# Query and forget tiles of a recurrent layer: the activations' high part and remainder as one wide operand, the two sums added by VectorE

## What is computed

```python
def hgrn2_mixer(h, w_in, lb, norm_g, w_out):
    u = h @ w_in
    q, fz, i, gate = jnp.split(u, 4, axis=-1)          # 256 x 2048 each
    log_f = jnp.logaddexp(jnp.log(lbf), jnp.log1p(-lbf) + jax.nn.log_sigmoid(fz))
    k = (1.0 - lbf) * jax.nn.sigmoid(-fz)
    ...
    # o_t = S_t^T q_t  with  S_t = diag(f_t) S_{t-1} + k_t v_t^T, in chunks
    o = hgrn2_chunk_scan(qc, kc, vc, bc)
    o = o * lax.rsqrt(jnp.mean(o * o, axis=-1, keepdims=True) + EPS)
    return (o * norm_g * jax.nn.silu(gate)) @ w_out
```

## Time and profile before

| | |
|---|---|
| median of 3 runs | 821.23 us (820.32 to 822.46) |
| the profiled execution | 821.18 us |
| its span | 819.9 us |
| TensorE busy | 801.5 us, 98% |
| VectorE busy | 627.7 us, 77% |
| ScalarE busy | 474.4 us, 58% |
| granted TensorE clock, mean | 0.997 |

### The profile page before, as it was taken

The page is one execution under the profiler, slowest core; times in us unless marked ns, Lnnn a source line. Parts: engine busy times, 40 slices in busy tenths (PEclk is TensorE's granted clock), DMA queues, the critical chain, the costliest instruction groups (busy, mean ns, idle before and its releaser), DMA issues.

```text
span 819.9 us, 12702 instructions
## 1 busy us (share of the span) xinstructions
PE 801.5 (98%) x5059; PEld 687.6 (84%) x5059; DVE 627.7 (77%) x939; ACT 474.4 (58%) x811; POOL 40.6 (5%) x52
## 2 busy tenths in 40 slices
PE   8999989999999999999999999999999999999996
PEld 5999978888998999999987789886476888888885
DVE  6786667747689889899795885898759877767775
ACT  6564444355667877868856551547636654455443
POOL 6010001700000000000000000000000000000000
PEclk9999999999999999999999999999999999999999
DMA  8989966594543444545346772936647655655631
GB/s 276 324 263 252 265 201 239 221 307 141 173 150 118 142 152 154 155 155 181 130 156 240 273 260 77 378 113 232 202 156 234 203 183 177 204 184 179 204 103 51
DMA packets 105701, 160.05 MB, mean 195 GB/s; under 512 B 11317, under 2 KB 74137, under 8 KB 103338
## 3 DMA queue, kind: packets, MB, share of 16 engines
q1 hardware_dynamic: 105642, 159.24, 59.1%
HBM read 156.02 MB, written 3.21 MB: 194 GB/s over the span
## 4 chain that ended last, share of the span: by engine, by line
PE 88%; DVE 6%; DMA 3%; ACT 2%; issue 1%; SPq 0%; DVEq 0%; ACTq 0%
PE acc L472 9%; PE acc L473 9%; PE acc L474 9%; PE acc L493 9%; PE acc L524 8%; PE acc L526 8%; PE acc L525 8%; PE acc L494 4%; PE misc L1322 3%; PE misc L2331 3%; PE misc L2333 2%; PE misc L2332 2%; PE misc L923 2%; DMA raw<-in_pool_w_in_dram 1%; PE acc L497 1%; PE misc L650 1%
## 5 line engine op out<-in xcount | busy, mean ns | idle before, releaser
L445 DVE TENSOR_TENSOR w_lo<-raw,w_hi 128x2048 fp32r<-128x2048 f32 x113 | 260.9, 2320 | 62.0 <-ACT w_hi L438 61.9
L438 ACT ACTIVATE w_hi<-raw 128x2048 fp32r<-128x2048 f32 x113 | 215.9, 1912 | 72.7 <-PE acc L526 16.9
L472 PE MATMUL acc<-X,w_hi 128*128 128x256 f32 x592 | 169.6, 286 | 3.1 <-DVE sg L1191 3.1
L473 PE MATMUL acc<-X,w_hi 128*128 128x256 f32 x592 | 168.1, 284 | 0.0
L474 PE MATMUL acc<-X,w_lo 128*128 128x256 f32 x592 | 168.0, 284 | 0.0
L472 PEld LDWEIGHTS acc<-X,w_hi 128*128 128x128 f32 x592 | 114.2, 193 | 7.8 <-DVE w_lo L445 4.0
L473 PEld LDWEIGHTS acc<-X,w_hi 128*128 128x128 f32 x592 | 114.2, 193 | 0.3
L474 PEld LDWEIGHTS acc<-X,w_lo 128*128 128x128 f32 x592 | 114.2, 193 | 0.0
L493 PE MATMUL acc<-X,w_hi 128*128 128x512 f32 x308 | 110.2, 397 | 0.0
L494 PE MATMUL acc<-X,w_lo 128*128 128x256 f32 x308 | 86.3, 280 | 0.0
L524 PE MATMUL acc<-w_hi,X 128*128 128x512 f32 (+1 forms) x176 | 69.3, 394 | 0.9 <-DVE w_lo L445 0.9
(11 more groups left out here) (304 smaller groups left out, 1493.9 us busy)
## 6 DMA issues: line engine op xcount, KB each, us to landing
raw<-in_hgrn_w_in_dram SPq DMA_DIRECT2D x32, 1024.0 KB, 5.7
ada_raw<-in_ada_w_dram SPq DMA_DIRECT2D x24, 1024.0 KB, 7.1
raw<-in_ffn_w_up_dram SPq DMA_DIRECT2D x22, 1024.0 KB, 5.1
raw<-in_pool_w_in_dram SPq DMA_DIRECT2D x15, 1024.0 KB, 7.6
raw<-in_ffn_w_down_dram SPq DMA_DIRECT2D x11, 1024.0 KB, 4.9
raw<-in_w_in_dram SPq DMA_DIRECT2D x10, 1024.0 KB, 6.3
raw<-in_pool_w_out_dram SPq DMA_DIRECT2D x8, 1024.0 KB, 5.1
raw<-in_hgrn_w_out_dram SPq DMA_DIRECT2D x8, 1024.0 KB, 5.1
```

The costliest lines, as they stand in the source:

```text
L438: self.hi_done.up(act.activation(self.w_hi[v % RING][:, 0:w], self.raw[j][:, 0:w], ACT.Copy), v)
L445: self.lo_done.up(dve.tensor_tensor(self.w_lo[j][:, 0:w], self.raw[j][:, 0:w], self.w_hi[v % RING][:, 0:w].bitcast(F32), ALU.subtract), v)
L472: pe.matmul(o, wh[:, k, c:c + P], xh[:, k, :], start=k == 0, stop=False)
L473: pe.matmul(o, wh[:, k, c:c + P], xl[:, k, :], start=False, stop=False)
```

## The change

The query and forget tiles of the recurrent layer are made by `project_wide` in place of `project`, 32 tiles in all. ScalarE copies the second half of the bank, VectorE adds the first half to that copy in place and gives the bank back. For a query tile ScalarE's copy was there before and read the only half. For a forget tile the copy is new: it goes into `sigma[1]`, VectorE adds to it, and then ScalarE takes both sigmoids from `sigma[1]`, where before it took them from the bank. VectorE's adds get places in its order: both query adds at the head of a pair, ahead of the masked copies of head 0; the first forget add between the two remainders of weights; the second behind them, ahead of the masked copies of head 1.

```diff
@@ pe_hgrn
             for h in range(2):
-                self.project(self.u_query[p], h, h * P, X, KD, self.both_ready("out") if p == h == 0 else None)
+                self.project_wide(self.u_query[p], h, h * P, self.both_ready("out") if p == h == 0 else None)
...
             for h in range(2):
-                self.project(self.u_forget[p], h, h * P, X, KD)
+                self.project_wide(self.u_forget[p], h, h * P)
@@ act_hgrn
-                self.freed(query, h, act.activation(self.queries_of(QK, h), acc[b][:, 0:TOK].rearrange("p (a t) -> p a t", a=2),
-                                                    ACT.Copy))
+                A.up(act.activation(self.queries_of(QK, h), acc[b][:, TOK:2 * TOK].rearrange("p (a t) -> p a t", a=2),
+                                    ACT.Copy), "query_rest", p, h)
...
-                act.activation(self.sigma[:, 0, :], acc[b][:, 0:TOK], ACT.Sigmoid, bias=0.0, scale=-1.0)
-                self.freed(forget, h, act.activation(self.sigma[:, 1, :], acc[b][:, 0:TOK], ACT.Sigmoid, bias=0.0))
+                z = self.sigma[:, 1, :]
+                A.up(act.activation(z, acc[b][:, TOK:2 * TOK], ACT.Copy), "forget_rest", p, h)
+                self.wait_freed(act, forget, h)
+                act.activation(self.sigma[:, 0, :], z, ACT.Sigmoid, bias=0.0, scale=-1.0)
+                t = A.up(act.activation(z, z, ACT.Sigmoid, bias=0.0))
                 l0, l1 = self.lb[:, 0, n:n + 1], self.lb[:, 1, n:n + 1]
-                self.wait_freed(act, forget, h)
+                act.wait_ge(A.h, t)
@@ dve
+    def dve_query_of(self, p, h):
+
+        dve, u, o = self.nc.vector, self.u_query[p], self.queries_of(self.QK[p % 2], h)
+        dve.wait_ge(self.A.h, self.A["query_rest", p, h])
+        main = self.acc[self.tiles_of[u][h][1]][:, 0:TOK].rearrange("p (a t) -> p a t", a=2)
+        self.freed(u, h, dve.tensor_tensor(o, o, main, ALU.add))
+
+    def dve_forget_of(self, p, h):
+        dve, u, z = self.nc.vector, self.u_forget[p], self.sigma[:, 1, :]
+        dve.wait_ge(self.A.h, self.A["forget_rest", p, h])
+        self.freed(u, h, dve.tensor_tensor(z, z, self.acc[self.tiles_of[u][h][1]][:, 0:TOK], ALU.add))
@@ dve_hgrn
-            else:
+            for h in range(2):
+                self.dve_query_of(p, h)
+            if p:
                 self.dve_scores_of(p - 1, 0)
...
                 self.lo(self.first(self.u_wide[p - 1], 1) + RING)
+            self.dve_forget_of(p, 0)
             self.lo(self.first(query) + RING)
             if p:
+                self.dve_forget_of(p, 1)
                 self.dve_scores_of(p - 1, 1)
...
+            else:
+                self.dve_forget_of(p, 1)
+            for h in range(2):
+                self.wait_freed(dve, query, h)
             self.levels(p)
```

## The result

The changed kernel takes 836.0 us (median of six runs; one of them took 2787.23 us, one of the kernel before 1126.41 in the session of e4 to e7 and one of e11 2026.03, which nothing here explains, and these three are left out of the ratios) against 821.12 for the kernel before: ratio 1.0178, 95% interval 1.0155 to 1.0201. The profiled execution took 835.99 us, its span 834.7, where the one before had 819.9.

What follows compares the result with a forecast made beforehand. The prediction took TensorE's queue, busy 98% of the span, as the bound. Stalls of 13.2 us less 1.8 saved gave +11.4 on 821.2, so 832.6 us; range 827 to 839, with 52% on 829 to 835.5.

Steps and rivals of the forecast that it cites:

- The tiles: Recurrent layer, TensorE: 32 tiles made with wider matmuls save 0.055 us each, 1.8 us in all.
- Pair 1: Second scores: TensorE stalls 3.36 us, as head 0's forget add stands behind masked copies and a remainder.
- The clock: Rival: pair 1's stall sends the clock to half speed, costing about 1.5 us, 834.1 us in all; 20%.
- Pair 2: Three existing waits (first scores, second scores, values) grow by the work added to their chains, 2.06 us in sum.
- Pairs 4 and 6: Before the values' second half TensorE waits for the last score copy on ScalarE, 1.75 us each.
- Pairs 3, 5, 7: Before the values' first half TensorE waits for VectorE's remainders of the turned heads, slack 0.41, stall 1.34 us each.
- After pair 7: Last values product, in the output stage: ScalarE's lateness is mostly hidden; 0.3 us taken.
- The add: Each VectorE add takes 0.42 us; at 0.34 about 1.3 us less in total, at 0.68 about 4 more.
- the rival with 838.6: The table load waits for the add, making each head 0 later, 6 us together: 838.6 us; 9%.
- Later stages give nothing back: Stages behind the layer: their loads are released by TensorE's progress and move with it, so no time is regained.
- The adds hide: Rival: ScalarE has the new round trips covered, so the 1.8 us saving shows alone: 819.4 us; 6%.
- Only pair 1 pays: Rival: the steady pairs absorb their lateness, leaving 3.4 + 0.3 - 1.8: 823.1 us, no change; 5%.

Runs made afterwards that it cites:

- e4: The changed kernel with pair 1's first forget add moved ahead of the masked score copies: 829.78 us, ratio 1.0103 to the kernel before.
- e7: The changed kernel with the edits of e4, e5 and e6 together: 824.97 us, ratio 1.0049 to the kernel before.
- e11: The kernel before with only query tiles wide, their adds later in pairs 2, 4 and 6, and the forget weights' split behind the score copies: 820.33 us.
- c_after: The changed kernel, unaltered, measured again in a later session: 832.54 us, ratio 1.0140 to the kernel before.
- e1: The kernel before with query and forget tiles wide but no adds, so part of the result is left out: 819.38 us, ratio 0.9981.
- e10: The kernel before with only the forget weights' split moved behind the score copies, nothing wide: 820.48 us, ratio 1.0003.
- after: The changed kernel in its first measurement and profile: 836.0 us, ratio 1.0178 to the kernel before.
- e3: The changed kernel with the query path as before, so only forget tiles are wide: 833.53 us, ratio 1.0151 to the kernel before.
- e5: The changed kernel with the query adds of pairs 2, 4 and 6 moved behind the first forget add: 833.65 us, ratio 1.0150 to the kernel before.
- e6: The changed kernel with head 1's forget copy made early into a buffer of its own: 831.29 us, ratio 1.0127 to the kernel before.
- e8: The changed kernel with the forget path as before and the query adds placed as in e5: 820.15 us, ratio 0.9988 to the kernel before.
- e9: e7 with the forget weights' split also moved behind the score copies on ScalarE: 820.54 us, ratio 0.9990 to the kernel before.
- e2: The changed kernel with the forget path as before, so only query tiles are wide: 821.46 us, ratio 1.0011 to the kernel before.

## Why the prediction was right, and where it was off

The direction and the places of the waits were right, and so was the mechanism, save for the clock and for what the odd pairs wait for. The sum, 11.4 us, is 2.6 short of the layer's growth. It is 3.4 short of the total's: 836.0 lies inside the range but above the 829 to 835.5 that had 52%. The 0.8 between the two is the late start less what the later stages gave back, which is chance in great part. It is chance too that c_after's median, 832.54, meets the forecast of 832.6. The 2.6 are made, to a tenth, of the clock 1.6, slower restarts behind waits 1.5 (below), the odd pairs 0.4 and pair 2 0.1, less 0.7 in the even pairs, 0.3 after pair 7 and 0.1 of tiles. Point by point:

- **The tiles, -1.8.** Measured -1.9 (e1, its longer waits taken out), 0.06 a tile. Right; the rows 2 and 3 by themselves give 0.05, the forecast took 0.055. The new tiles come 2.81 us apart after the change:

```profile
340.11 0.39 PE L493 MATMUL acc<-X,w_hi 128*128 128x512 f32 x1
...
342.92 0.40 PE L493 MATMUL acc<-X,w_hi 128*128 128x512 f32 x1
```

- **Pair 1, 3.36.** Idle 3.36. e4 shows the cause: the add's place behind the masked copies and a remainder. That the two agree to the last digit is luck, since idle leaves out some 0.2 of lateness (below).
- **The clock.** Taken only as a rival, at 20% and 1.5 us. It happened, for 1.6 us: TensorE is 236.45 - 231.57 = 4.88 us later than before when pair 1's second scores begin, and 240.12 - 233.59 = 6.53 at the last matmuls of that block, which is the same work. Of the steps, this one was decided wrongly, though the price was right. The case of the earlier trace rows was one; the five profiles here with a stall of 3.36 to 3.49 in pair 1 all had it. The table of the Trainium skill, "TensorE: Matmul & The Clock Gate", section "Why this matters for your kernels", says that idle gaps between bursts of matmuls bring the half clock back; the trace agrees with it at these five stalls.
- **Pair 2, 2.06.** 2.16 more idle measured: 0.15 in front of the first scores, 0.79 at the second, 1.22 at the values.
- **Pairs 4 and 6, 1.75 each.** Idle 1.38 and 1.43, lateness 1.66. The chain was as forecast: from odd-pair product to even-pair product TensorE's way grew to 394.23 - 363.88 = 30.35 us, against 28.69 that its own work takes.
- **Pairs 3, 5, 7, 1.34 each.** 1.49, 1.48, 1.49. What is late is not what I named. I read the slack from the heads' remainders, which end 0.41 us ahead. The last thing wanted is a copy of scores, in the row that I passed over. Timeline before and after, pair 5:

```profile
350.62 0.28 ACT L1358 ACTIVATE AT<-misc 128x128 f32<-128x128 f32 x1
```

```profile
362.50 1.13 DVE L1451 SCALAR_TENSOR_TENSOR ML_b<-misc,table,MH_b 128x128 fp32r<-128x128 f32 x4 [2.81 <-ACT MH_b L1441]
...
363.59 0.28 ACT L1358 ACTIVATE AT<-misc 128x128 f32<-128x128 f32 x1
```

  Before, the copy ended at 350.90 and TensorE began at 351.06: slack 0.16, not 0.41. After, the remainders end at 363.63 and the copy at 363.87, and TensorE begins at 363.88. With 0.16 the term is 1.60 + 0.11 - 0.16 = 1.55 each, 0.6 more for the three. By the same row even pairs start with TensorE 0.25 and not 0.04 behind the remainders, which takes 0.2 off each of them. The sign named for these pairs, a wait for the heads' remainders, did not come true: the remainders end first. How far each of the two would have held TensorE by itself is read from the times; no run separates them.
- **After pair 7, 0.3.** Nothing was seen there. **The add,** 0.42: right, and so is its cover by the table load in head 0 (the rival with 838.6 falls). What it holds of VectorE is 232.52 - 232.19 = 0.33 (the remainder behind it starts at 232.52), so the upper price of 0.68 falls too; the two rows that gave 0.34 and 0.68 do not read the accumulator, as the add does.
- **Later stages give nothing back.** Wrong by about 1: before, TensorE waits for a remainder of weights at this place, after it does not (in c_after 0.31):

```profile
525.15 0.50 PE L524 MATMUL acc<-w_hi,X 128*128 128x512 f32 x1 [0.94 <-DVE w_lo L445]
```

  The stages behind the layer took 382.8 us before, 381.7 after, 381.8 to 383.0 in the others: partly chance, so I give it no firm figure.
- **Missing from the sum:** about 1.5 us. Idle added 12.8, the tiles took 1.9 and the clock added 1.6, which makes 12.5; the layer grew by 14.0. Where TensorE starts again its first matmuls come slower. Behind the wait that ended at 363.88 (its row is above):

```profile
364.18 0.39 PE L1374 MATMUL misc<-VT,AT 128*128 128x128 f32 x2
364.40 0.39 PE L1375 MATMUL misc<-VT,AT 128*128 128x128 f32 x2
```

  The second step comes 0.30 us behind the first and the third 0.22 behind that. That is 0.08 a wait; besides, idle is counted from the modelled end of the last matmul (0.39 where the next one usually comes after 0.23), which hides some 0.17. So 0.25 a wait, and the six new waits (pairs 1 and 3 to 7) make the 1.5 that are missing. e10 agrees: it removes one wait, of 0.32, from the kernel before,

```profile
265.05 0.49 PE L1373 MATMUL misc<-VT,AT 128*128 128x128 f32 x2 [0.32 <-ACT AT L1358]
```

  and its layer is 0.56 us shorter with 0.31 less idle. How the 0.25 divides between the two parts is worked out, not measured.
- **The rivals.** "The adds hide" falls: e1 is its time, with the adds the layer is 15.5 us longer. "Only pair 1 pays" falls: e4 without that stall is still 8.9 us above before.

In all, the shift of two steady pairs was forecast at 2.7 us. From 303.57 to 363.88 they take 60.31 us where before they took 57.40 (293.66 to 351.06), 2.9 more. No wait for weights came up in the layer, so that sign of being wrong did not show.

## What to carry to other kernels

Where TensorE is 98% busy, merging matmuls saves little (0.06 us a tile here). A round trip between ScalarE and VectorE put ahead of a result that TensorE waits for is paid in full once the slack there is used up, though VectorE is idle for 23% and ScalarE for 43% of the span. Read the slack for each consumer, as the end of each of its inputs against its start, and take the last, not the busiest: place new work where nobody waits behind it, and move work with slack (here a split of weights) behind the urgent copies. Where a new stall comes near one that was followed by a half clock before, put the clock into the forecast.

## What the runs showed of the chip

- The granted clock went to 0.50 for 3.41 us behind every idle of 3.36 to 3.49 us in pair 1, in five profiled executions (after, c_after, e3, e5, e6), and in none of the kernels without that stall. In the pooling stage, where all runs idle at about 108 us, it went to 0.50 after idles of 2.59 to 3.87 us, for 3.41 or 6.83 us, and stayed full after 1.59 (e1) and 0.38 (e8). Shorter idles were followed by it too, near 14.7 us into the span: 1.88 to 2.35 us in five profiles (after, e5, e9, e10, e11), while idles of 1.21 to 1.75 at the same place in the other nine were not. The layer's waits of 1.38 to 1.59 never were. The pooling row of after and the one of e8:

```profile
110.17 0.35 PE L472 MATMUL acc<-X,w_hi 128*128 128x256 f32 x1 [3.07 <-DVE sg L1191]
```

```profile
105.77 0.36 PE L472 MATMUL acc<-X,w_hi 128*128 128x256 f32 x1 [0.38 <-DVE sg L1191]
```

- That pooling idle moves by itself between profiles of kernels whose code there is the same; it and the half clock behind it are part of why layers that differ by 2 us give totals that can't be told apart.
- A wait costs TensorE some 0.25 us beyond its idle (above; e10 removes one of 0.32 and gains 0.56). A short wait can show as no idle at all: e2 loses 0.2 us in pair 4 and in pair 6 that no list of waits has.
